# Moving the last input rotation behind the low parts of the pooled branch in a pool and state-space block

## What is computed

```python
h = rmsnorm(x, norm_pre) * (1 + scale) + shift
u_pool, z_pool, u_ssm, z_ssm, g_pool, g_ssm = split(h @ w_in)
# mixer A: trailing means over 2, 4, 8, 16 tokens minus the token, a linear map per group
y_pool = (einsum(pooled(u_pool), pool_w) * pool_scale) * silu(z_pool)
# mixer B: a complex diagonal state space (associative scan), gelu, sigmoid GLU
y_ssm = glu(gelu(Re(C x) + D u)) * silu(z_ssm)
merged = sigmoid(g_pool) * (y_pool @ w_branch_pool) + sigmoid(g_ssm) * (y_ssm @ w_branch_ssm)
out = x + gate * rmsnorm(merged @ w_out, norm_post)
```

## Time and profile before

| | |
|---|---|
| median of 3 runs | 955.61 us (955.01 to 956.26) |
| the profiled execution | 956.41 us |
| its span, first to last instruction | 954.6 us |
| TensorE matmuls, busy | 931.8 us, 98% |
| VectorE, busy | 639.8 us, 67% |
| ScalarE, busy | 350.2 us, 37% |
| granted TensorE clock, mean | 0.999 |

### The profile page before, as it was taken

One profiled execution on the slowest core, in us unless ns is written; L12 is line 12 of the kernel. 1 busy time (PEld: TensorE's weight loads), 2 busy tenths in 40 slices (PEclk: granted clock), 3 DMA queues, 4 the chain that ended last, 5 costly groups with the idle time before them and its releaser, 6 DMA issues.

```text
span 954.6 us, 11609 instructions
## 1 busy us (share of the span) xinstructions
PE 931.8 (98%) x4408; PEld 782.6 (82%) x4408; DVE 639.8 (67%) x916; ACT 350.2 (37%) x455; POOL 45.3 (5%) x82
## 2 busy tenths in 40 slices
PE   3999999999999999999999999999999999999997
PEld 3888888888888888888888888888888888888885
DVE  5988899877788887437898789755344444455233
ACT  5851353334444444434444436341022231223111
POOL 0019800000000000000000000000000000000000
PEclk9999999999999999999999999999999999999999
DMA  9843355445555444556899682597543258422222
GB/s 346 303 141 117 127 200 181 155 154 193 179 180 203 152 172 155 188 136 180 226 242 227 133 199 92 159 324 269 184 165 111 89 224 188 161 89 89 89 88 89
DMA packets 95719, 164.60 MB, mean 172 GB/s; under 512 B 38576, under 2 KB 55088, under 8 KB 95664
## 3 DMA queue, kind: packets, MB, share of 16 engines
q1 hardware_dynamic: 86304, 159.40, 52.3%
q10 hardware_dynamic: 9360, 4.46, 1.9%
HBM read 116.64 MB, written 47.19 MB: 172 GB/s over the span
## 4 chain that ended last, share of the span: by engine, by line
PE 94%; DVE 2%; SPq 1%; DMA 1%; ACT 1%; issue 0%; DVEq 0%
PE ps L1943 47%; PE ps L2063 20%; PE ps L2185 9%; PE psb L2063 8%; PE ps L2134 2%; PE psb L2114 1%; PE psa L2021 1%; PE psa L1943 1%; PE psb L2123 1%; PE psa L2102 1%; PE psb L1971 1%; DMA x_tok<-in_x 1%; DMA taps<-k_d 1%; PE ps L1971 0%; SPq L867 0%
## 5 line engine op out<-in xcount | busy, mean ns | idle before, releaser
L1943 PE MATMUL ps<-bop,w_hi 128*128 128x512 f32 x1120 | 300.7, 390 | 1.2 <-issue 1.0
L1943 PEld LDWEIGHTS ps<-bop,w_hi 128*128 128x128 f32 x1120 | 209.2, 188 | 44.5 <-issue 1.7
L1943 PE MATMUL ps<-bop,w_lo 128*128 128x512 f32 x560 | 172.4, 389 | 0.0
L1943 PEld LDWEIGHTS ps<-bop,w_lo 128*128 128x128 f32 x560 | 105.1, 188 | 21.9
L1399 DVE TENSOR_TENSOR w_lo<-raw,w_hi 128x1024 fp32r<-128x1024 f32 x43 | 53.2, 1237 | 47.3 <-ACT w_hi L1019 47.1
L2063 PE MATMUL ps<-bop,r_hi 128*128 128x512 f32 x272 | 83.7, 389 | 0.0
L1019 ACT ACTIVATE w_hi<-raw 128x1024 fp32r<-128x1024 f32 x43 | 45.3, 1053 | 70.9 <-PE ps L1943 56.3
L2063 PEld LDWEIGHTS ps<-bop,r_hi 128*128 128x128 f32 x272 | 51.1, 188 | 10.6
L2063 PE MATMUL ps<-t_hi,r_hi 128*128 128x512 f32 x140 | 55.0, 393 | 0.0
L2063 PE MATMUL ps<-t_hi,r_lo 128*128 128x512 f32 x140 | 54.6, 390 | 0.0
L2063 PE MATMUL ps<-t_lo,r_hi 128*128 128x512 f32 x140 | 54.5, 389 | 0.0
(11 more groups left out here) (318 smaller groups left out, 1580.0 us busy)
## 6 DMA issues: line engine op xcount, KB each, us to landing
raw<-in_wstream SPq DMA_DIRECT2D x52, 512.0 KB, 5.2
pair_raw<-in_wstream SPq DMA_DIRECT2D x26, 512.0 KB, 4.2
ada<-in_w_ada SPq DMA_DIRECT2D x16, 512.0 KB, 11.2
x_tok<-in_x SPq DMA_DIRECT2D x8, 512.0 KB, 6.7
gs_d<-gt SPq DMA_DIRECT2D x8, 512.0 KB, 5.0
win_d<-win_new SPq DMA_DIRECT2D x8, 512.0 KB, 2.7
wout_d<-wout_new SPq DMA_DIRECT2D x8, 512.0 KB, 3.8
wout<-wout_d SPq DMA_DIRECT2D x8, 512.0 KB, 4.8
```

What stands on the lines that cost most here:

```text
L1943: last = mm(ps[slot(u)][:, f * HALF:f * HALF + HALF], a[:, k, :], b(k, f), start=k == order[0] and q == 0, stop=k == order[-1] and q == 2)
```

## The change

On VectorE, in the last turn, the two first `in_low` and the `rotate_in(7)` are taken out of the turn. Behind the turns all eight `in_low` now run in one loop, with `yp_out(6)` between those of tile 1 and tile 2 and `yp_out(7)` behind that of tile 3, and `rotate_in(7)` comes after them, directly ahead of the loop over `bp`. No other engine's program changes.

```diff
                 split_lo(USE["up", m] + 2)
                 if m == KT - 1:
                     pool_low(m)
-                    in_low(0)
-                    in_low(1)
-                rotate_in(m)
                 if m < KT - 1:
+                    rotate_in(m)
                     scans(m)
                     pool_low(m)
...
-            yp_out(6)
-            for n in range(2, KT):
+            for n in range(KT):
                 in_low(n)
-                if n == 3:
+                if n == 1:
+                    yp_out(6)
+                elif n == 3:
                     yp_out(7)
+            rotate_in(KT - 1)
```

## The result

The changed kernel took 956.49 us in the median of 16 runs (955.84 to 959.07), the kernel before 955.40 beside it. The ratio is 1.0016, with a 95% interval of 1.0009 to 1.0023: 0.9 to 2.2 us more, 1.5 in the middle. The two medians differ by less, 1.1. One of the 16 executions of the kernel before took 2462 us, for a reason that nothing here shows, and counts in no ratio. The profiled execution took 955.95, with a span of 954.1. The times of the changed kernel are not spread evenly: 11 lie between 955.8 and 956.9, five between 958.2 and 959.1, and none between.

What follows compares the result with a forecast made beforehand. TensorE, 94% of the span, was taken to bound the kernel, with 1 us to win; +1.16 at bp 1 and +1.54 at bp 3 summed to +2.7, from 955.61 to 958.3 us, range 956.6 to 959.6.

Steps and rivals of the forecast that it cites:

- What bounds it: Whole kernel: TensorE is 94% of the span, nearly without holes; 1 us to win, any new hole reaches the end.
- steps (1): In front of bp 0: yp_out(6) runs earlier, the hole goes, and bp 0 begins 1.15 us earlier.
- (2): VectorE after 591: two new waits, 1.15 for the product and 1.75 for ScalarE, make it 2.90 us later; no hole inside bp 0.
- Step (3): In front of bp 1: the weights split comes behind rotate_in(7), a hole of 2.3 us; TensorE is 1.16 later than before.
- Step (4): At the last state product: rotation out, 2.90 us later, stays hidden behind the taps with 1.8 to spare.
- Step (5): SP's DMA queue: the burst starts 2.90 us later, zs 0 lands as much later; bp 3 gets a hole of 1.44.
- the second hole: In front of bp 3, from the late landing of zs 0: 1.44 us and 0.10 for the slow first step.
- the lower of the two bounds: Landing of zs 0 later by +1.16 us, if its issue alone counts; the upper, queue alone, is +2.90.
- the margin of 0.30: In front of bp 3 before the change: its weights split, behind the landing of zs 0, was ready 0.30 us early.
- Rival C: Behind the hole of 2.3 TensorE's clock falls, costing some 2.7 us; total +3.2 to +5.4, chance 0.10.
- rival B: Only the hole in front of bp 1, zs 0 not held by the queue: +1.2 to +2.1 us, chance 0.37.
- A: The forecast itself: holes in front of both bp 1 and bp 3, +2.2 to +3.2 us, chance 0.46.

Runs made afterwards that it cites:

- the longer holes: Changed kernel with one or two more VectorE multiplications ahead of the split of bp 1's weights: 959.35 us (ratio 1.0042) and 960.30 us (1.0050).
- the woven one: Changed kernel with the last rotation's two multiplications behind in_low(2), yp_out(7) behind in_low(4), bp 1's weights split behind in_low(7), then the rotation's sum: 954.22 us, ratio 0.9988.
- the weights first: Changed kernel with the split of the weights of bp 1 ahead of the last rotation: 955.45 us, ratio 0.9995.
- the multiplication alone: Kernel before with only yp_out(6) moved ahead of the rotation: 955.72 us, ratio 1.0001.
- the late burst: Kernel before with two more VectorE multiplications (2.5 us) between the split of the weights of bp 1 and the last scans: 955.54 us, ratio 1.0001.

## Why the prediction was right or wrong

*What bounds it, and steps (1) and (2): right.* The hole in front of `bp` 0 went, worth 1.16 (forecast 1.15). VectorE waits 1.02 and 1.72 in two places (forecast 1.15 and 1.75, counted from the place where it could have gone on).

*Step (3): right.* A hole in front of `bp` 1, 2.12 long (forecast 2.3 from the start of one matmul to the start it should have had; the profile's 2.12 leaves the overlap out, and counted the forecast's way it is 606.72 - 604.44 = 2.28), and TensorE 1.20 late behind it (forecast 1.16). The run with the split ahead of the rotation shows that the split's place is the cause. Step (4), the rotation out hidden behind the taps, held too.

*Step (5): wrong.* It said that the landing of `zs` 0 follows the burst, because the DMA queue has work all the time and a store ahead of it was in flight when `zs` was issued. From this came the second hole, 1.54 of the forecast's 2.7. It measured 0 in the profile of the changed kernel:

```profile
615.16 0.80 SPq L939 DMA_DIRECT2D y_raw<-y_d  x2
...
622.28 0.32 SPq L934 DMA_DIRECT2D zs_t<-zs_d  x1
```

```profile
zs_t<-zs_d SPq DMA_DIRECT2D x1, 512.0 KB, 5.5
```

Against TensorE (the last pair of pooled tile 6, at 590.13 here and 591.79 before) the burst starts 2.92 later, as forecast, and `zs` is issued 1.20 later; but it lands only some 0.7 later, less than the lower of the two bounds.

The queue did not have work all the time: before, it had nearly run out when `zs` came. From the start of the burst to the issue of `zs`, SP's queue moved this much before (613.90 to 622.74) and in the changed kernel (615.16 to 622.28), with packets, MB, and share of the 16 engines:

```profile
q1 hardware_dynamic: 684, 2.53, 85.3%
```

```profile
q1 hardware_dynamic: 487, 1.80, 76.0%
```

The burst is five transfers of 512 KB, 2.62 MB. So before, nearly all of its data had moved when `zs` was issued, though the landing of its last store was still 2.4 us away: that late landing was no sign of a backlog. In the microsecond behind the issue of `zs` the same queue moved 0.07 MB, and ScalarE's stores of y (q10) took over half of the engines' time:

```profile
q10 hardware_dynamic: 344, 0.16, 53.8%
```

What held `zs` up before is thus more likely these stores, which move with TensorE; no run separates them. A burst that comes later first eats up a slack. In all ten profiles `zs` landed behind the store: by 1.4 to 1.8 us where it was issued 5.5 to 7.1 us after the start of the burst, by 2.0 to 3.6 where it was 8.0 to 9.9. Counted from its issue it took 7.2 us in the profile with the least time between (5.46, with 1.36 MB moved), where the margin of 0.30 in front of `bp` 3 did break, 5.2 to 5.8 at 6.3 to 7.1, and 3.6 to 6.0 at 8.0 and more. The rule of the Trainium skill ("DMA: Bandwidth & Descriptors", "Queues, rings and completion order") that the prediction put beside it speaks of the order of service, and the order held in every profile; the error was to take the order for a length.

*Rival C, the clock: underrated.* "2.3 lies nearer to 1.0" was the reason for 0.10. The hole of 2.1 let the clock fall in something like a third of the executions. Its price there, 1.6 in the one profile that caught it, is smaller than the 2.7 forecast, which the longer holes do show. The 2.7 itself was read from the pace of matmuls at the start; the view of windows has a granted clock of 1.00 there, and its record of the clock begins only near 20.9, so the pace alone shows that stretch.

So most executions, and with them the median of 956.5, show rival B's mechanism, one hole and +1.2; the upper third shows a smaller C, +2.8 in the one profile. The difference of 1.5 in the middle lies in B's range (+1.2 to +2.1), not in A's (+2.2 to +3.2). The forecast of 958.3 lies beside the upper group by chance: it had the second mechanism wrong. The sign held. The range of 956.6 to 959.6 was counted from a median before of 955.61; the ratio puts the changed kernel at 957.1 on that, inside it by rival B, while the 956.49 as measured, beside 955.40, lies 0.1 below its edge. And 0.16% more is below the 0.2% that I gave as the bound of what can be told, which had the chance of 0.37, not the 0.60 of slower.

## What to carry to other kernels

Where one engine is nearly always busy, look for the late item in front of each of its waits and move only that one; what is moved behind a run of others must be weighed against the next item that the busy engine asks for, here a weights split with 1.95 us of lead against a lateness of 2.90. A wait on the helper engine is a place to put work into: the same three operations, two of them woven into a wait of 1.7 and the third behind the split, turned 1.5 us lost into 1.1 won. A late landing doesn't say that the queue is full; the bytes that it had moved by then do. And a hole of TensorE has a price beyond its length, which has to be read from many executions, because one profile may show either case.

## What the runs showed of the hardware

- The clock of TensorE fell to its lower level behind a hole of 2.1 us in one profile and not in two others; by the times it did so in some executions and not in others (12 of 38 above 958). Behind 3.4 and 4.6 both profiles show the fall, and nine of ten runs paid 0.8 to 3.4 us extra. With no hole over 1.0 us, none of the 44 runs of the four other kernels (the woven one, the weights first, the multiplication alone, the late burst) took over 956.5.
- The low stretch lasted 3.4 us in one profile and 6.8 in two, and cost 1.60, 2.79 and 2.67. It began 2.3, 2.5 and 3.6 us after TensorE had stopped; behind the last matmul of the kernel it began 4.4 us later in one profile and 2.8 in another.
- A hole costs more than its length even with the clock at full: behind one of 0.4 the next two steps took 1.50 and 1.39 where 1.36 is usual.
- A 512 KB load behind a burst of five such transfers in one queue landed behind the last of them in all ten profiles, and moving the burst 2.5 us closer to it did not delay it: 6.3 us or 8.8 us after the start of the burst it landed 5.8 or 6.0 after its issue; at 5.5 us it took 7.2, at 9.8 and 9.9 only 3.6 and 3.9.
- A landing can come well after the data: 2.53 of a burst's 2.62 MB had moved 2.4 us before its last store landed.
- Why the upper group had 5 of 16, 2 of 11 and 5 of 11 members, what the times between the two groups are, and what sets the moment of the fall, stays open.
